# First feed-forward up projection as Strassen block products, 15 of 16 pairs of output tiles

## The chip, the cores and the metric

The kernel runs on 1 core of one Trainium2 chip. The metric is the device time of one execution, in microseconds (us). Engines: PE is TensorE, DVE is VectorE, ACT is ScalarE, POOL is GpSimd, SP is SyncE, which issues the weight loads.

## The reference

Two transformer-like layers over 512 tokens of width 1024. Only the first layer's feed-forward part is touched:

```python
h2 = rms_norm(x, norm2_w)
x = x + jnp.square(jax.nn.relu(h2 @ w_ff_in)) @ w_ff_out      # D_FF = 4096
```

All is fp32. The kernel holds activations transposed: 128 channels on the partitions, 512 tokens along the free side, so a 1024-channel activation is 8 tiles of 128x512.

## The kernel before

Every large product is a "job": one packed 128x1024 fp32 weight block (512 KB) makes one 128x512 output tile. Precision comes from splitting every factor into a rounded high part and the rest (low): a job is 8 row tiles (kt) times three matmuls, high by high, high by low, low by high, 24 matmuls of 512 columns into one PSUM bank (`block_of`, L344 to L346, called by `job`). A weight block passes four engines: SP loads it into one of four `raw` slots (L291); ACT writes the high part (`split`, L1009, 128x1024); POOL subtracts, in four pieces of 128x256 (L312); PE uses both. All queues are in order; the program is written by hand, one instruction list per engine, tied by counting semaphores.

The part around the change, in order:

- Eight jobs of the output projection (`J_OUT`). After each, DVE adds the PSUM tile to `x` (`add_to_x`), ACT squares it and makes the high part of the next input `b_hi`, DVE adds the square to `acc` and makes `b_lo` (`prep`).
- 64 feed-forward jobs: four groups g, each 8 up jobs (inputs `b_hi`, `b_lo`) and 8 down jobs (inputs `a_hi`, `a_lo`). The norm's factor `rstd` is applied after the up product: after the first up job PE sums `acc` (`norm_sum`), ACT takes the root, DVE the reciprocal (`norm_inverse`), and in the middle of the second up job (`norm_job`) PE spreads it over the partitions and ACT copies it to `rstd` (`take_rstd`). After each up job (`ff_hidden`) DVE computes relu times rstd from PSUM, ACT squares it twice, DVE subtracts to get `a_lo`. After each down job DVE adds the PSUM tile to `x` (`ff_down`).
- Then the first jobs of the second layer.

## Time and profile before

| | us |
|---|---|
| median of 3 runs | 1589.41 (1589.36 to 1590.12) |
| the profiled execution | 1589.58 |
| its span, first to last instruction | 1587.4 |
| PE busy | 1571.9 (99%) |
| POOL busy | 799.1 (50%) |
| DVE busy | 706.8 (45%) |
| ACT busy | 684.2 (43%) |

The busy time of an engine is the union of its instructions. The span is what the trace covers; the execution's own time is 2.2 us more. Matmuls overlap in the pipeline, so the duration of one (389 ns for 512 columns) is longer than the spacing of their starts, which is what counts.

### The profile page before, as it was taken

Reading aid. Unit: us, or ns where it says so; the run is one execution under the profiler, and the core shown is the slowest. Engines: PE = TensorE matmul, PEld = TensorE weight load, DVE = VectorE, ACT = ScalarE, POOL = GpSimd, SP = SyncE. Lnnn points to the kernel's source line nnn. Section 1 sums busy time; section 2 is a strip of 40 time slices with the busy share of each in tenths; the row PEclk is TensorE's granted clock in tenths of the full one; section 3 lists DMA queues with packets and bytes.
Section 4 is the critical chain, followed back from the end, with each engine's and each line's share of the span. In section 5 each row is a group of like instructions: output and inputs, shape, how many; then the busy total and the mean of one; then the engine's idle time right before and its main releaser. Section 6 shows DMA issues by size and latency. Waiting matters only on the chain. (4 is left out here: it accounts for less than half of the span.)

```text
span 1587.4 us, 22464 instructions
## 1 busy us (share of the span) xinstructions
PE 1571.9 (99%) x7602; PEld 1267.0 (80%) x7602; DVE 706.8 (45%) x1363; ACT 684.2 (43%) x1112; POOL 799.1 (50%) x1060
## 2 busy tenths in 40 slices
PE   9999999999999999999999999999999999999998
PEld 6677777777888888888887887778988888888886
DVE  5496986664233212121132446653333651552354
ACT  6435786554334423232233434543643442342333
POOL 6344654333455454545455532256544555556553
PEclk9999999999999999999999999999999999999999
DMA  5322222113232232223232421133322233233231
GB/s 196 97 94 72 86 82 75 59 57 118 94 104 93 93 106 93 94 92 106 92 106 94 132 80 53 50 111 112 114 90 96 80 106 106 80 106 106 80 106 66
DMA packets 46133, 149.91 MB, mean 94 GB/s; under 512 B 4649, under 2 KB 9905, under 8 KB 46065
## 3 DMA queue, kind: packets, MB, share of 16 engines
q1 hardware_dynamic: 39648, 140.00, 27.2%
q10 hardware_dynamic: 6416, 8.98, 1.7%
q8 instruction: 45, 0.74, 0.2%
q14 instruction: 24, 0.19, 0.0%
HBM read 146.73 MB, written 2.11 MB: 94 GB/s over the span
## 5 line engine op out<-in xcount | busy, mean ns | idle before, releaser
L312 POOL TENSOR_TENSOR w_lo<-w_raw,w_hi 128x256 fp32r<-128x256 f32 x1056 | 798.9, 789 | 765.6 <-ACT w_hi L1009 765.0
L1009 ACT ACTIVATE w_hi<-w_raw 128x1024 fp32r<-128x1024 f32 x264 | 274.9, 1051 | 293.5 <-PE job L346 284.0
L344 PE MATMUL job<-a_hi,w_hi 128*128 128x512 f32 (+1 forms) x986 | 382.4, 388 | 0.6 <-DVE a_lo L1584 0.6
L346 PE MATMUL job<-a_hi,w_lo 128*128 128x512 f32 (+1 forms) x986 | 377.3, 383 | 0.0
L345 PE MATMUL job<-a_lo,w_hi 128*128 128x512 f32 (+1 forms) x986 | 377.1, 382 | 0.0
L344 PE MATMUL job<-b_hi,w_hi 128*128 128x512 f32 x936 | 369.0, 394 | 0.8 <-DVE sq L1587 0.5
L346 PE MATMUL job<-b_hi,w_lo 128*128 128x512 f32 x936 | 364.7, 390 | 0.0
L345 PE MATMUL job<-b_lo,w_hi 128*128 128x512 f32 x936 | 364.4, 389 | 0.0
L344 PEld LDWEIGHTS job<-a_hi,w_hi 128*128 128x128 f32 x986 | 185.3, 188 | 54.8 <-issue 13.0
L346 PEld LDWEIGHTS job<-a_hi,w_lo 128*128 128x128 f32 x986 | 185.4, 188 | 36.3
L345 PEld LDWEIGHTS job<-a_lo,w_hi 128*128 128x128 f32 x986 | 185.5, 188 | 34.7
L344 PEld LDWEIGHTS job<-b_hi,w_hi 128*128 128x128 f32 x936 | 175.8, 188 | 40.4 <-issue 4.6
L346 PEld LDWEIGHTS job<-b_hi,w_lo 128*128 128x128 f32 x936 | 175.7, 188 | 36.8
L345 PEld LDWEIGHTS job<-b_lo,w_hi 128*128 128x128 f32 x936 | 175.9, 188 | 35.4 <-issue 0.2
L1587 DVE TENSOR_TENSOR arena<-arena,job 128x512 f32<-128x512 f32 (+2 forms) x89 | 60.5, 680 | 253.4 <-PE job L346 247.4
L1584 DVE SCALAR_TENSOR_TENSOR arena<-arena,vec 128x512 f32<-128x512 f32 x112 | 100.2, 895 | 60.8 <-ACT arena L1522 53.0
L1587 DVE TENSOR_TENSOR arena<-job,rstd 128x512 f32<-128x512 f32 x100 | 68.7, 688 | 130.8 <-PE job L346 108.2
L1024 ACT ACTIVATE sq<-arena 128x512 f32<-128x512 f32 x47 | 29.6, 631 | 109.4 <-DVE arena L1587 108.4
L1522 ACT ACTIVATE arena<-arena,vec 128x512 f32<-128x512 f32 x44 | 35.6, 809 | 87.4 <-DVE arena L1587 87.4
L1587 DVE TENSOR_TENSOR a_lo<-arena,a_hi 128x512 f32 (+1 forms) x58 | 40.0, 692 | 62.9 <-ACT a_hi L1270 42.2
L1269 ACT ACTIVATE arena<-arena 128x512 f32<-128x512 f32 x32 | 20.2, 632 | 106.5 <-DVE arena L1584 106.5
L1584 DVE SCALAR_TENSOR_TENSOR arena<-job,rstd 128x512 f32<-128x512 f32 x32 | 22.1, 691 | 91.2 <-PE job L346 86.6
(340 smaller groups left out, 1482.3 us busy)
## 6 DMA issues: line engine op xcount, KB each, us to landing
w_raw<-w_all SPq DMA_DIRECT2D x264, 512.0 KB, 3.4
arena<-x_t ACTq DMA_DIRECT2D x8, 512.0 KB, 5.9
out_t<-arena SPq DMA_DIRECT2D x6, 256.0 KB, 2.1
arena<-rg_w ACTq DMA_DIRECT2D x1, 1024.0 KB, 8.0
arena<-mem_t ACTq DMA_DIRECT2D x1, 1024.0 KB, 6.6
spare<-row_table ACTq DMA_DIRECT2D x3, 256.0 KB, 4.2
...
```

The lines of the kernel that those rows point to most:

```text
L312: nc.gpsimd.tensor_tensor(w_lo[:, sl, c], raw[:, sl, c], w_hi[:, sl, c].bitcast(F32), ALU.subtract).then_inc(s("lo_ready"), 1)
L344: mm(ps[:, 0:n], w_hi[:, sl, c], hi[:, kt, 0:n], start=kt == 0, stop=False)
L345: mm(ps[:, 0:n], w_hi[:, sl, c], lo[:, kt, 0:n], start=False, stop=False)
L346: ins = mm(ps[:, 0:n], w_lo[:, sl, c], hi[:, kt, 0:n], start=False, stop=kt == last)
L1009: fn(w_hi[:, sl], raw[:, sl], ACT.Copy).then_inc(s("hi_ready"), 1)
L1024: fn(sq[:, f % 2, :], src, ACT.Square).then_inc(s("sq_ready"), 1)
L1269: fn(act_s[:, c % 2, :], act_t[:, c % 2, :], ACT.Square).then_inc(s("ff_sq"), 1)
L1522: fn(f_c[u], f_u[u][:, PAD:PAD + T], ACT.Identity, scale=vcol("conv_w2", col + 88), bias=vcol("conv_b2", col)).then_inc(s("f_head"), 1)
L1584: return v.scalar_tensor_tensor(out=out_, in0=a, scalar=sc, in1=b, op0=op0, op1=op1)
L1587: return v.tensor_tensor(out_, a, b, op)
```

## The change

The first two up jobs stay as they are. The other 30 are taken in 15 pairs n (two output tiles of 128 channels). A pair's weights are a 2x2 block matrix (output tile 1 or 2, row tiles 0 to 3 or 4 to 7; W11, W12 the two tiles' upper rows, W21, W22 their lower rows), its input is a 2x2 block matrix as well (row tiles 0 to 3 or 4 to 7, token halves of 256). Seven block products in Strassen's manner (Winograd's form) take the place of eight. One block product is 4 row tiles times three matmuls of 256 columns (`ff_product`).

- Weight sums T1 = W12 - W11, T2 = W22 - T1, T3 = W22 - W12, T4 = W21 - T2 are made by POOL (`ff_sum`), each 128x512.
- Unit of weights is now 128x512 (a half of a slot): ACT makes its high part (`ff_high`), POOL the low part of raw blocks (`ff_low`, now one instruction), DVE the low part of the sums (`sum_low`). There are eight units in `w_hi` and `w_lo`; the high part of a unit waits until PE has used the one eight before. W12 alone is never multiplied.
- Input sums are made once, in four steps `combine(q)` on DVE after the last three output jobs and after the reciprocal; ACT makes their high part (`s_high`), DVE the low part.
- Output sums: three PSUM regions of 256 columns; ACT copies intermediates out (`copy_u1`, `copy_u2`, `copy_p5`) before PE adds on, DVE adds (`c11`, `c12`, `c22`), and `activate` makes the hidden tiles.
- PE's order interleaves a pair with the next: T2, W22, T3 of pair n, W11 of the next, T4 of n, W21 and T1 of the next. Pairs form four chains (1 to 3, 4 to 7, 8 to 11, 12 to 15); 8 down jobs stand between chains, and the first two down jobs are interleaved with the chain's end, on three PSUM banks in turn.
- The 64 jobs leave the numbering (`J_IN2` is now 73) and loops are written out.

```diff
+FF_JOBS = 64
+FF_CHAINS = ((1, 2, 3), (4, 5, 6, 7), (8, 9, 10, 11), (12, 13, 14, 15))
+def ff_job(n):
+    return 16 * (n // 4) + 2 * (n % 4)
+def ff_units():
+    order = [("job", 0, 0), ("job", 0, 1), ("job", 1, 0), ("job", 1, 1), None, None, None]
+    for g, chain in enumerate(FF_CHAINS):
+        order += [(w, chain[0]) for w in ("W11", "W21", "T1")]
+        for n, nxt in zip(chain, chain[1:]):
+            order += [("T2", n), ("W22", n), ("T3", n), ("W11", nxt), ("T4", n), ("W21", nxt), ("T1", nxt)]
+        n, d = chain[-1], 16 * g + 8
+        order += [("T2", n), ("W22", n), ("T3", n), ("job", d, 0), ("T4", n), ("job", d + 1, 0)]
+        order += [("job", d, 1), ("job", d + 1, 1)]
+        order += [("job", d + e, half) for e in range(2, 8) for half in range(2)]
+    return order
...
+        f_t = tiles(20, 8).rearrange("p (a i) c -> p a i c", a=2)
+        f_mid = [tiles(28, 2), spare[:, 0:2, :]]
+        f_xw = spare[:, 2, :]
+        f_s = [flat(t).rearrange("p (c t) -> p c t", t=256) for t in (tiles(28, 2), spare[:, 0:2, :])]
...
+            def ff_raw_free(f):
+                if f % 16 >= 8 or f < 2:
+                    sp.wait_ge(s("ff_raw_low"), FF_RAW["job", f, 1])
+                elif f % 2 == 0:
+                    sp.wait_ge(s("ff_sum"), FF_SUM["T4", 4 * (f // 16) + f % 16 // 2])
+                else:
+                    sp.wait_ge(s("ff_raw_low"), FF_RAW["W22", 4 * (f // 16) + f % 16 // 2])
+            for f in range(FF_JOBS):
+                if f < SLOTS:
+                    sp.wait_ge(s("lo_ready"), (J_IN2 + f - SLOTS + 1) * PIECES)
+                else:
+                    ff_raw_free(f - SLOTS)
+                sp.dma_start(ff_raw(f), w_all[J_IN2 + f]).then_inc(raw_landed[(J_IN2 + f) % SLOTS], 16)
...
+            def ff_low(*tag):
+                pool.wait_ge(s("ff_high"), FF_HIGH[tag])
+                nc.gpsimd.tensor_tensor(ff_tile(w_lo, tag), ff_source(tag), ff_tile(w_hi, tag).bitcast(F32),
+                                        ALU.subtract).then_inc(s("ff_raw_low"), 1)
+            def ff_sum(w, n, a, b):
+                if n >= 3:
+                    pool.wait_ge(s("ff_sum_low"), FF_SUMMED[w, n - 2])
+                if w in ("T2", "T4"):
+                    pool.wait_ge(s("ff_sum"), FF_SUM[w, n] - 1 if w == "T2" else FF_SUM["T2", n])
+                nc.gpsimd.tensor_tensor(ff_source((w, n)), a, b, ALU.subtract).then_inc(s("ff_sum"), 1)
...
+                for n in chain:
+                    for f in (ff_job(n), ff_job(n) + 1):
+                        pool.wait_ge(raw_landed[(J_IN2 + f) % SLOTS], 16 * ((J_IN2 + f) // SLOTS + 1))
+                    ff_sum("T1", n, ff_block("W12", n), ff_block("W11", n))
+                    ff_low("W11", n)
+                    ff_sum("T2", n, ff_block("W22", n), ff_source(("T1", n)))
+                    ff_low("W21", n)
+                    ff_sum("T3", n, ff_block("W22", n), ff_block("W12", n))
+                    ff_sum("T4", n, ff_block("W21", n), ff_source(("T2", n)))
+                    ff_low("W22", n)
...
+            def ff_product(w, n, ps, xs, first):
+                ff_wait(w, n)
+                wh, wl = ff_tile(w_hi, (w, n)), ff_tile(w_lo, (w, n))
+                for kt in range(4):
+                    c, (xh, xl) = slice(kt * P, kt * P + P), xs(kt)
+                    mm(ps, wh[:, c], xh, start=first and kt == 0, stop=False, skip_group_check=True)
+                    mm(ps, wh[:, c], xl, start=False, stop=False, skip_group_check=True)
+                    ins = mm(ps, wl[:, c], xh, start=False, stop=kt == 3, skip_group_check=True)
+                ins.then_inc(s("ff_used"), 1)
...
+            def ff_p3(n):
+                pe.wait_ge(s("ff_copied"), FF_COPY["P5", n])
+                ff_product("W22", n, ff_regions(n)[2], s_part(3), False)
+            def ff_p4(n):
+                pe.wait_ge(s("ff_part"), FF_PART["C22", n])
+                ff_product("T4", n, ff_regions(n)[0], x_part(4, 256), False)
+            def ff_p5(n):
+                if n == 1:
+                    pe.wait_ge(s("ff_part"), FF_PART["rests", 3])
+                ff_product("T1", n, ff_regions(n)[2], s_part(0), True)
+            def ff_p6(n):
+                pe.wait_ge(s("ff_copied"), FF_COPY["U1", n])
+                ff_product("T2", n, ff_regions(n)[0], s_part(1), False)
+            def ff_p7(n):
+                pe.wait_ge(s("ff_copied"), FF_COPY["U2", n])
+                ff_product("T3", n, ff_regions(n)[0], s_part(2), False)
...
+            for g, chain in enumerate(FF_CHAINS):
+                ff_p1(chain[0])
+                ff_p2(chain[0])
+                ff_p5(chain[0])
+                for n, nxt in zip(chain, chain[1:]):
+                    ff_p6(n)
+                    ff_p3(n)
+                    ff_p7(n)
+                    ff_p1(nxt)
+                    ff_p4(n)
+                    ff_p2(nxt)
+                    ff_p5(nxt)
+                ff_p6(chain[-1])
+                ff_p3(chain[-1])
+                ff_p7(chain[-1])
+                down(g, 0, 0).then_inc(s("ff_used"), 1)
+                ff_p4(chain[-1])
+                down(g, 1, 0).then_inc(s("ff_used"), 1)
+                down(g, 0, 1, (4, 5))
+                down(g, 1, 1, (4, 5))
+                down(g, 0, 1, (7, 6)).then_inc(s("ff_used"), 1)
+                down(g, 1, 1, (7, 6)).then_inc(s("ff_used"), 1)
+                for d in range(2, 8):
+                    for half in range(2):
+                        down(g, d, half).then_inc(s("ff_used"), 1)
...
+            def ff_high(*tag):
+                u = FF_UNIT[tag]
+                if tag[0][0] == "T":
+                    act.wait_ge(s("ff_sum"), FF_SUM[tag])
+                else:
+                    f = tag[1] if tag[0] == "job" else ff_job(tag[1]) + int(tag[0][2]) - 1
+                    act.wait_ge(raw_landed[(J_IN2 + f) % SLOTS], 16 * ((J_IN2 + f) // SLOTS + 1))
+                if u >= 8 and FF_ORDER[u - 8]:
+                    act.wait_ge(s("ff_used"), FF_USED[FF_ORDER[u - 8]])
+                else:
+                    act.wait_ge(s("job_done"), J_IN2 - SLOTS + u % 8 // 2 + 1)
+                fn(ff_tile(w_hi, tag), ff_source(tag), ACT.Copy).then_inc(s("ff_high"), 1)
...
+            def s_high(q):
+                act.wait_ge(s("ff_part"), FF_PART["sums", q])
+                fn(s_hi[:, :, q * 256:q * 256 + 256], f_s[q % 2], ACT.Copy).then_inc(s("ff_high"), 1)
+            def square(n, c):
+                act.wait_ge(s("ff_part"), FF_PART["act", n, c])
+                fn(act_s[:, c, :], act_t[:, c, :], ACT.Square)
+                fn(a_hi[:, 2 * (n % 4) + c, :], act_t[:, c, :], ACT.Square).then_inc(s("fhi_ready"), 1)
...
+            ff_high("W21", 1)
             norm_root(2)
-            split(J_FF + 4)
+            ff_high("T1", 1)
             take_rstd(2)
-            for c in range(8):
-                if c >= 2:
-                    split(J_FF + 3 + c)
-                ff_hidden(c % 4, 0, c // 4)
-            with act.Fori(0, 2) as i:
-                for c in range(4):
-                    split(J_FF + 11 + c, i)
-            with act.Fori(1, 3) as g:
-                with act.Fori(0, 2) as i:
-                    for c in range(4):
-                        split(J_FF + 3 + c, g * 4 + i)
-                        ff_hidden(c, g, i)
-                with act.Fori(0, 2) as i:
-                    for c in range(4):
-                        split(J_FF + 11 + c, g * 4 + i)
-            with act.Fori(0, 2) as i:
-                for c in range(4):
-                    split(J_FF + 3 + c, i + 12)
-                    ff_hidden(c, 3, i)
-
+            s_high(3)
+            ff_high("T2", 1)
+            square(0, 0)
+            square(0, 1)
...
+                ff_high("W22", a)
+                ff_high("T3", a)
+                ff_high("W11", b)
+                ff_high("T4", a)
+                copy_u1(a)
+                ff_high("W21", b)
+                ff_high("T1", b)
+                copy_p5(a)
+                for i, n in enumerate(chain[:-1]):
+                    nxt, after = chain[i + 1], chain[i + 2] if i + 2 < len(chain) else None
+                    ff_high("T2", nxt)
+                    copy_u2(n)
+                    ff_high("W22", nxt)
+                    ff_high("T3", nxt)
+                    ff_high("W11", after) if after else ff_high("job", d, 0)
+                    copy_u1(nxt)
+                    square(n, 1)
+                    ff_high("T4", nxt)
+                    ff_high("W21", after) if after else ff_high("job", d + 1, 0)
+                    square(n, 0)
+                    copy_p5(nxt)
+                    ff_high("T1", after) if after else ff_high("job", d, 1)
...
+            def combine(q):
+                part, xw = f_s[q % 2], f_xw
+                lower, upper = slice(0, 256), slice(256, T)
+                did(ts(xw, x[:, q, :], vcol("norm2", q)))
+                settle()
+                did(stt(part[:, 0], x[:, q + 4, upper], vcol("norm2", q + 4), xw[:, upper], ALU.mult, ALU.add))
+                did(tt(part[:, 2], xw[:, lower], xw[:, upper], ALU.subtract))
+                settle()
+                did(tt(part[:, 1], part[:, 0], xw[:, lower], ALU.subtract))
+                settle()
+                stt(part[:, 3], x[:, q + 4, lower], vcol("norm2", q + 4), part[:, 1], ALU.mult,
+                    ALU.subtract).then_inc(s("ff_part"), 1)
+                dve.wait_ge(s("ff_part"), FF_PART["sums", q])
+                dve.wait_ge(s("ff_high"), FF_HIGH["S", q])
+                c = slice(q * 256, q * 256 + 256)
+                tt(s_lo[:, :, c], part, s_hi[:, :, c].bitcast(F32), ALU.subtract).then_inc(s("ff_part"), 1)
...
+                if f >= 5:
+                    combine(f - 5)
...
+            def sum_low(*tag):
+                dve.wait_ge(s("ff_high"), FF_HIGH[tag])
+                tt(ff_tile(w_lo, tag), ff_source(tag), ff_tile(w_hi, tag).bitcast(F32), ALU.subtract).then_inc(
+                    s("ff_sum_low"), 1)
...
+            def c22(n):
+                part = f_mid[n % 2][:, 1, 256:T]
+                dve.wait_ge(s("ff_copied"), FF_COPY["P5", n])
+                dve.wait_ge(s("ff_used"), FF_USED["T3", n])
+                tt(part, part, ff_regions(n)[0], ALU.add).then_inc(s("ff_part"), 1)
...
+            def activate(n):
+                dve.wait_ge(s("ff_part"), FF_PART["C22", n])
+                dve.wait_ge(s("fhi_ready"), 2 * n)
+                stt(act_t[:, 1, :], f_mid[n % 2][:, 1, :], 0.0, rstd[:], ALU.max, ALU.mult).then_inc(s("ff_part"), 1)
+                stt(act_t[:, 0, 0:256], f_mid[n % 2][:, 0, 0:256], 0.0, rstd[:, 0:256], ALU.max, ALU.mult)
+                dve.wait_ge(s("ff_used"), FF_USED["T4", n])
+                stt(act_t[:, 0, 256:T], ff_regions(n)[0], 0.0, rstd[:, 256:T], ALU.max, ALU.mult).then_inc(
+                    s("ff_part"), 1)
...
+            dve.wait_ge(s("norm_root"), 2)
+            v.reciprocal(rcol[:, :, 0], rcol[:, :, 0]).then_inc(s("norm_inv"), 1)
+            combine(3)
+            dve.wait_ge(s("rstd_ready"), 2)
+            first_hidden(0)
+            sum_low("T1", 1)
+            first_hidden(1)
+            hidden_low(0, 0)
+            hidden_low(0, 1)
...
+                for i, n in enumerate(chain[:-1]):
+                    nxt, after = chain[i + 1], chain[i + 2] if i + 2 < len(chain) else None
+                    sum_low("T2", nxt)
+                    c12(n)
+                    sum_low("T3", nxt)
+                    c22(n)
+                    activate(n)
+                    hidden_low(n, 1)
+                    c11(nxt)
+                    sum_low("T4", nxt)
+                    hidden_low(n, 0)
+                    if after:
+                        sum_low("T1", after)
```

The names below: `w_hi`, `w_lo` are weight parts, `arena` and `spare` hold `x`, the sums and the intermediates, `s_hi`, `s_lo` the input sums' parts, `score` and `turn` are the PSUM regions.

DVE at the end of the output jobs, from the last output job's addition on. Before:

```order
L1587 TENSOR_TENSOR arena<-arena,job 128x512
L1587 TENSOR_TENSOR acc<-acc,sq 128x512
L1584 SCALAR_TENSOR_TENSOR b_lo<-arena,vec,b_hi 128x512
L1606 RECIPROCAL rcol<-rcol 128x4
L1584 SCALAR_TENSOR_TENSOR arena<-job,rstd 128x512
L1587 TENSOR_TENSOR a_lo<-arena,a_hi 128x512
```

With the change, from `combine(1)` (after the last but one addition) to the reciprocal:

```order
L1945 TENSOR_SCALAR spare<-arena,vec 128x512
L1938 SCALAR_TENSOR_TENSOR spare<-arena,vec,spare 128x256
L1941 TENSOR_TENSOR spare<-spare 128x256 x2
L1938 SCALAR_TENSOR_TENSOR spare<-arena,vec,spare 128x256
L1941 TENSOR_TENSOR s_lo<-spare,s_hi 128x4x256
L1941 TENSOR_TENSOR arena<-arena,job 128x512
L1941 TENSOR_TENSOR acc<-acc,sq 128x512
L1938 SCALAR_TENSOR_TENSOR b_lo<-arena,vec,b_hi 128x512
...
L1941 TENSOR_TENSOR s_lo<-arena,s_hi 128x4x256
L2304 RECIPROCAL rcol<-rcol 128x4
```

Each `combine` stands ahead of the next output job's addition or of the reciprocal.

ACT at the start of the first chain, from the input sums' last high part to the first copy out of PSUM (before, two pairs of squares stood right behind the `rstd` copy):

```order
L1560 ACTIVATE s_hi<-spare 128x4x256
L1555 ACTIVATE w_hi<-arena 128x512
L1565 ACTIVATE arena<-arena 128x512
L1566 ACTIVATE a_hi<-arena 128x512
L1565 ACTIVATE arena<-arena 128x512
L1566 ACTIVATE a_hi<-arena 128x512
L1555 ACTIVATE w_hi<-w_raw 128x512
L1555 ACTIVATE w_hi<-arena 128x512
L1555 ACTIVATE w_hi<-w_raw 128x512
L1555 ACTIVATE w_hi<-arena 128x512
L1570 ACTIVATE spare<-score 128x256
```

The last row is `copy_u1(1)`, for which PE's product T2 of pair 1 waits.

POOL within a chain: where there were four pieces of one split per job, one pair now has

```order
L446 TENSOR_TENSOR arena<-w_raw 128x512
L437 TENSOR_TENSOR w_lo<-w_raw,w_hi 128x512
L446 TENSOR_TENSOR arena<-w_raw,arena 128x512
L437 TENSOR_TENSOR w_lo<-w_raw,w_hi 128x512
L446 TENSOR_TENSOR arena<-w_raw 128x512
L446 TENSOR_TENSOR arena<-w_raw,arena 128x512
L437 TENSOR_TENSOR w_lo<-w_raw,w_hi 128x512
```

seven instructions of 128x512, in the order T1, W11, T2, W21, T3, T4, W22.

## Rows read from the trace of the kernel before

**Rows 1.** The page: busy time and granted clock.

```profile
PE 1571.9 (99%) x7602; PEld 1267.0 (80%) x7602; DVE 706.8 (45%) x1363; ACT 684.2 (43%) x1112; POOL 799.1 (50%) x1060
...
PEclk9999999999999999999999999999999999999999
```

**Rows 2.** Timeline of PE in an up or down job: start us, us, engine, line.

```profile
559.82 0.39 PE L344 MATMUL job<-a_hi,w_hi 128*128 128x512 f32 x1
...
566.84 0.39 PE L345 MATMUL job<-a_lo,w_hi 128*128 128x512 f32 x1
```

**Rows 3.** Timeline of PE, products of 256 columns.

```profile
1124.78 0.28 PE L346 MATMUL job<-a_hi,w_lo 128*128 128x256 f32 x1
...
1127.90 0.28 PE L875 MATMUL job<-w_hi,a_lo 128*128 128x256 f32 x1
```

**Rows 4.** Timeline of PE, first matmuls of 256 columns after others.

```profile
1098.24 0.36 PE L344 MATMUL job<-a_hi,w_hi 128*128 128x256 f32 x1
1098.44 0.28 PE L345 MATMUL job<-a_lo,w_hi 128*128 128x256 f32 x1
```

**Rows 5.** Groups of DVE by form: xcount | busy us, mean ns | idle before.

```profile
L1587 DVE TENSOR_TENSOR a_lo<-arena,a_hi 128x512 f32 x44 | 30.5, 693 | 51.7 <-ACT a_hi L1270 32.4 <-ACT a_hi L1527 19.3
L1591 DVE TENSOR_SCALAR arena<-arena,small 128x512 f32<-128x512 f32 x17 | 8.3, 487 | 0.6
L1587 DVE TENSOR_TENSOR arena<-job,arena 128x256 f32<-128x256 f32 x8 | 3.4, 424 | 21.3 <-PE job L346 19.0 <-ACT arena L1019 2.3
```

**Rows 6.** Groups of ACT by form.

```profile
L1009 ACT ACTIVATE w_hi<-w_raw 128x1024 fp32r<-128x1024 f32 x264 | 274.9, 1051 | 293.5 <-PE job L346 284.0 <-issue 7.3 <-DMA w_raw<-w_all 0.9
L1270 ACT ACTIVATE a_hi<-arena 128x512 f32 x24 | 14.8, 616 | 0.0
```

**Rows 7.** Timeline of ACT, a copy of 256 columns out of PSUM.

```profile
1100.75 0.38 ACT L1019 ACTIVATE arena<-turn 128x256 f32<-128x256 f32 x1 [1.13 <-PE turn L385]
```

**Rows 8.** Groups of POOL, feed-forward stretch 490 to 860 us.

```profile
L312 POOL TENSOR_TENSOR w_lo<-w_raw,w_hi 128x256 fp32r<-128x256 f32 x272 | 191.9, 737 | 179.8 <-ACT w_hi L1009 179.8
```

**Rows 9.** Timeline of POOL, one split while DVE reads PSUM or rests.

```profile
474.84 2.83 POOL L312 TENSOR_TENSOR w_lo<-w_raw,w_hi 128x256 fp32r<-128x256 f32 x4 [2.61 <-ACT w_hi L1009]
```

**Rows 10.** Timeline where DVE (two inputs in SBUF) and POOL overlap.

```profile
155.07 1.12 DVE L1584 SCALAR_TENSOR_TENSOR arena<-arena,vec 128x512 f32<-128x512 f32 x1
...
155.60 1.18 POOL L312 TENSOR_TENSOR w_lo<-w_raw,w_hi 128x256 fp32r<-128x256 f32 x1
```

**Rows 11.** Busy time of POOL by stretch: us, busy us (x pieces).

```profile
130.00:200.00 70.00, 43.24 (x43) 1.00 0.23 76
466.00:860.00 394.00, 204.19 (x290) 1.00 0.30 97
```

**Rows 12.** Timeline of DVE, last output jobs and the reciprocal.

```profile
493.60 0.69 DVE L1587 TENSOR_TENSOR arena<-arena,job 128x512 f32<-128x512 f32 x1 [2.64 <-PE job L346]
...
499.05 0.69 DVE L1587 TENSOR_TENSOR arena<-arena,job 128x512 f32<-128x512 f32 x1 [2.64 <-PE job L346]
...
504.48 0.69 DVE L1587 TENSOR_TENSOR arena<-arena,job 128x512 f32<-128x512 f32 x1 [2.64 <-PE job L346]
...
506.54 0.74 DVE L1584 SCALAR_TENSOR_TENSOR b_lo<-arena,vec,b_hi 128x512 fp32r<-128x512 f32 x1
510.94 0.18 DVE L1606 RECIPROCAL rcol<-rcol 128x4 f32<-128x4 f32 x1 [3.66 <-ACT rcol L1014]
```

**Rows 13.** Timeline of ACT, root of the norm.

```profile
507.42 1.28 ACT L1014 ACT_TABLE_LOAD   x1
510.64 0.27 ACT L1014 ACTIVATE rcol<-o,cst 128x4 f32<-128x4 f32 x1 [1.94 <-PE o L374]
```

**Rows 14.** Timeline of PE, first up job, norm sum, spread.

```profile
504.21 0.39 PE L344 MATMUL job<-b_hi,w_hi 128*128 128x512 f32 x1
...
509.66 0.95 PE L374 MATMUL o<-cst,acc 128*128 128x2 f32 x8
...
514.01 1.05 PE L385 MATMUL turn<-cst,rcol 128*128 128x128 f32 x8
```

358 lines of the change are left out of this document (266 added, 92 removed).

## The prediction

 The duration of a matmul is no price, since matmuls overlap; the price is the spacing of their starts. 31 spacings of 512 columns take 566.84 - 559.82 = 7.02 us, 0.2265 each [rows 2]; 26 spacings of 256 columns take 3.12 us, 0.1200 each [rows 3]. Then I read what the engines that feed PE can do in the time of a pair: DVE and ACT [rows 5 to 7], POOL alone [rows 8, 9], POOL against DVE [rows 10, 11], and the chain around the norm before the first pair [rows 12 to 14].
>
> **PE work.** A pair was 48 matmuls of 512 columns, 48 x 0.2265 = 10.87 us. It becomes 7 x 12 = 84 of 256 columns, 84 x 0.1200 = 10.08 us. An eighth fewer columns gives only 7%, since each start has some 13 ns that don't shrink (2 x 0.1200 - 0.2265). The saving is 0.79 us a pair, 15 x 0.79 = **11.9 us**. That is everything the change can win.
>
> The Trainium skill ("TensorE: Matmul & The Clock Gate", Back-to-back issue gap) gives the isolated gap as N / 2.4 + 2.5 ns. By it 48 x 215.8 - 84 x 109.2 ns would be 1.19 us a pair, an estimate of 17.8 us in all. The rows show 226.5 and 120.0 ns, so the measurement decides and the sum doesn't use it.
>
> **The input sums before the first pair.** One `combine` is a scale of 512 columns (0.49), four operations of 256 (0.42 as the row of that width shows, a little more for those with a factor), each but one waiting for the one before: 2.3 us. Then ACT's high part of 1024 columns, 1.05 [rows 6], then DVE's low part, twice 0.69 less one start, 1.25 [rows 5]. In all 4.6 us, and DVE's in-order queue stands still for ACT in it. An output job's own DVE work runs from the addition to the end of `b_lo` 2.8 us (504.48 to 507.28), the jobs come every 5.44 [rows 12], and 2.8 + 4.6 is 7.4. So the addition of 499.05 moves to 501.0, that of 504.48 to 508.4, the last `b_lo` to 511.2, and to 512.2 with what POOL takes from DVE (below). PE wants it for the last row tile of the first up job, 21 matmuls after 504.21 [rows 14], at 509.0: a wait of 3.2. Next, `combine(2)`, the high part, a weight split of 0.55, the table load and root of 1.28 + 0.27 [rows 13] bring the reciprocal from 510.94 to 517.85, against a wish of PE at 517.2: 0.65. `combine(3)` stands ahead of the first hidden tile, and that ahead of T1's low part, ready at 524.6; PE wants it at 523.3: 1.3. The last is on ACT: behind both hidden tiles' squares (done at 526.4) stand four splits of 0.55 and then `copy_u1(1)`, 0.38 [rows 6, 7], done at 529.0. PE's product T2 waits for it from 526.0: 3.0. The front costs 3.2 + 0.65 + 1.3 + 3.0 = **8.15 us**; without POOL's disturbance 6.5, with more of it 9.
>
> **POOL's pace.** Per pair of jobs POOL had 8 pieces of 256 columns, 8 x 0.71 = 5.7 us [rows 9]. Now it has 7 instructions of 512: three low parts and four sums. None of this width is in the trace. Bounds: two whole pieces, 2 x 0.737 = 1.47; and two spacings of 2.83 / 4 = 0.71 less one start of 0.15, as DVE saves it between 256 and 512 columns (0.424 and 0.693) [rows 5], 1.26. I take 1.30, nearer to the low end, as there is one start where there were two. Then DVE. POOL's piece takes 0.737 in the whole feed-forward stretch [rows 8], where DVE's operations read PSUM or fall into POOL's pauses. Where DVE reads two operands from SBUF, a piece takes 1.18 and the DVE operation 1.12 [rows 10], so each is held up by about 0.45; in the stretch 130 to 200 us a piece takes 43.24 / 43 = 1.0 [rows 11]. A pair has six low parts of this kind (four of sums, two of hidden tiles) and one and a half relu operations, 7.5 of 512 columns: at most 7.5 x 0.45 = 3.4 us. POOL is never idle there, so I count 0.8 of it, 2.7. A pair then costs POOL 7 x 1.30 + 2.7 = 11.8 us, 1.69 an instruction, against PE's 10.08. POOL falls behind inside a chain and catches up in the down jobs (there 2.8 of each 5.44 us).
>
> How far ahead it starts is limited by the eight unit buffers: PE at t = 0 ends the down jobs; W21 of the second pair may be split only when PE has used W11 of the first (1.44), at 2.6. From there it is the 16th POOL instruction that makes T3 of the fourth pair. Behind it come ACT's split, DVE's low part, and, in the same DVE queue, `c22` of the third pair, for which PE's T4 waits: 2.5 us. PE wants it after 21 products of 1.44 us, at 30.2. 2.6 + 16 x 1.69 + 2.5 = 32.1: **1.9 us** per chain, three chains 5.7. In the first chain there is no lead: POOL starts W22 of the first pair at 527.0, T3 of the third is its 13th, 527.0 + 22.0 + 2.5 = 551.5, and PE, from 529.0, wants it 11 products later at 544.8: **6.6 us**, in several waits (`copy_u2` behind T2's split, `c22` behind T3's low part).
>
> **What is hidden.** ACT: seven splits of 0.55, three copies of 0.38 and four squares of 0.6 are 7.4 us of 10.08. The SP queue loads the same blocks, two per pair, into four slots that come free a pair earlier than needed. The down jobs' interleaving gives `activate` of the last pair 5 us of PE work as cover; without it some 3 us per chain would be bare. That DVE's low parts are no longer hidden for POOL is counted above.
>
> **The sum.** -11.9 + 8.15 + 6.6 + 5.7 = +8.5. On the profiled execution's 1589.58 (0.2 above the median) this is **1598 us**. Low end: front 6.5, POOL at 1.26 without collisions (first chain 1, others 0): -4.4, 1585. High end: POOL at 1.47 + 0.48 = 1.95, first chain 11, others 6.6 each, front 9: +28, 1617. What a measurement of this kernel can tell from no change is 0.2%, 3.2 us.
>
> **Rivals.**
>
> 1. *POOL keeps up, faster.* If collisions are rare because DVE's operations fall between POOL's, the other chains have no wait (this decides at 1.57 us an instruction) and the first little: 1585. For it: 0.737 in rows 8. Against: POOL had pauses then and has none now.
> 2. *DVE becomes the bound.* What holds DVE in rows 10 is one piece of 256; for 512 it would be 0.45 + 0.55 = 1.0, and eight such operations a pair, 8 x 1.65 + 1.7 = 15 us, exceed even POOL. Twenty of them lie before the decisive `c22` of a chain: 37 + 1 us against 30.2, 7.5 each; the first chain 15; with the front: -11.9 + 8.2 + 15 + 22.5 = +34, 1623. Against: an operation that finds POOL between two instructions, or follows one of DVE's own, doesn't wait. The rule behind it is in the Trainium skill ("SBUF — State Buffer", Who interferes with whom): whoever issues first has the shared ports for the whole instruction, and the other fully blocks.
> 3. *The products don't do what they promise.* After other work the second matmul of 256 columns started 0.20 after the first, 0.08 late [rows 4]. If each of the 105 products began so, 8.4 us of the saving would be gone and, with the waits, the time 1606.
> 4. *No change*: front as forecast, POOL between 1.5 and 1.6 an instruction, 1588 to 1592.
>
> **How the numbers follow.** Forecast (POOL behind, 1593 to 1615) 0.56; rival 1 0.18; rival 2 0.10; rival 3 0.05; rival 4 0.11. Range 1585 to 1616: it leaves out rival 2 and half of rival 1. Slower 0.71, same 0.11, faster 0.18. The slower cases' own range is 1593 to 1618.
>
> **What would show it.** Right: matmuls of 256 columns with 0.12 between starts; before the first pair PE idle some 8 us, by `b_lo`, the spread, T1's low part and the copy out of PSUM; POOL 90% busy or more within chains at 1.6 to 1.8 an instruction; PE waiting late in each chain for DVE's addition, and early not at all. Wrong: POOL's mean under 1.5, or PE idle in the first chain under 5 us (rival 1); DVE low parts of 1.5 us and more (rival 2); starts 0.2 apart at each product's head (rival 3).

## The result, and the profile after

The change is slower: 1610.45 us, median of 4 (1610.06 to 1612.12), against 1589.47 (1589.36 to 1590.12) for the kernel before beside it. The ratio is 1.0134 [1.0121, 1.0147]: +21 us where the prediction had +8.5.

The page of the kernel after, busy time and three of its rows of tenths (a slice is 40 us):

```profile
span 1608.3 us, 23172 instructions
PE 1570.0 (98%) x8142; PEld 1290.3 (80%) x8142; DVE 844.5 (53%) x1507; ACT 739.8 (46%) x1270; POOL 872.8 (54%) x977
PE   9999999999998799999999999999999999999998
DVE  5496986654336837455473435744233651452354
PEclk9999999999999999999999999999999999999999
```

PE lost only 2 us of busy time where [rows 1] and the predicted saving ask for 12, and two slices are no longer full. The row of the clock shows nothing at this width: 9 is "90% or more". The same stretch in pieces, as start:end, length, then busy us (xcount) of PE, PEld, DVE, ACT, POOL, then the granted clock, shows it:

```profile
490.00:504.00 14.00, 14.00 (x63) 11.61 (x62) 8.54 (x13) 6.03 (x10) 6.04 (x5) 1.00 0.21 72
504.00:514.00 10.00, 5.39 (x24) 4.13 (x22) 7.95 (x11) 2.82 (x4) 4.50 (x3) 1.00 0.18 52
514.00:520.00 6.00, 5.75 (x18) 4.89 (x19) 3.90 (x9) 3.51 (x5) 1.89 (x2) 0.54 0.01 1
520.00:525.00 5.00, 5.00 (x25) 4.19 (x24) 3.98 (x5) 1.46 (x3) 2.83 (x2) 0.87 0.20 57
...
620.00:630.00 10.00, 10.00 (x87) 10.00 (x86) 10.00 (x9) 7.21 (x14) 10.00 (x7) 1.00 0.26 81
630.00:640.00 10.00, 7.32 (x49) 7.12 (x48) 8.88 (x11) 4.22 (x9) 8.84 (x7) 0.83 0.32 103
```

Two things are there: PE idle (4.6 us in 504 to 514, 2.7 in 630 to 640), and right behind each idle time a clock of 0.54, 0.87, 0.83. In the trace the granted clock goes to its lower level (1.2 instead of 2.4 GHz) from 514.46 to 521.28 and, for 3.41 us each, at 555.42, 633.92, 722.67 and 811.41. Each time PE had just waited 2.7 to 4.9 us and had taken up work again. What PE waits for between 490 and 900 us, by releaser (total, times, longest):

```profile
PE score L792 <- DVE spare L1941: 9.5, 4, 2.7
PE job L781 <- DVE b_lo L1938: 4.9, 1, 4.9
PE score L792 <- DVE arena L1941: 3.8, 4, 3.0
PE score L792 <- DVE w_lo L1941: 2.1, 1, 2.1
PE score L792 <- ACT spare L1574: 1.7, 1, 1.7
PE turn L792 <- ACT spare L1578: 0.3, 1, 0.3
```

The waits sum to 22.2 us. All but 2.0 us end with DVE. The account of PE's time closes: -11.9 saved + 22.2 waits + half of 20.5 us at half clock (6.83 + 4 x 3.41), 10.2, is **+20.5**; the spans differ by 1608.3 - 1587.4 = 20.9. Two of its terms are rough and nearly cancel. At the lower clock the spacing is 0.213 instead of 0.120 (512 columns: 0.427 instead of 0.2265), so a fall of 3.41 us costs 1.5 to 1.6 and not 1.7. And an idle time is 0.16 short, since the matmul before it counts as busy for 0.28 where its spacing is 0.12. With both, the account gives +21.4. It says where PE's time went, not what would be won if one term were gone; that is left to the experiments.

One wait and what follows it on PE, the timeline (start, us; the bracket is the idle time before and its releaser):

```profile
630.23 0.28 PE L793 MATMUL score<-b_lo,w_hi 128*128 128x256 f32 x1
630.35 0.28 PE L794 MATMUL score<-b_hi,w_lo 128*128 128x256 f32 x1
633.31 0.39 PE L792 MATMUL score<-b_hi,w_hi 128*128 128x256 f32 x1 [2.68 <-DVE spare L1941]
633.53 0.28 PE L793 MATMUL score<-b_lo,w_hi 128*128 128x256 f32 x1
...
634.27 0.42 PE L792 MATMUL score<-b_hi,w_hi 128*128 128x256 f32 x1
634.49 0.41 PE L793 MATMUL score<-b_lo,w_hi 128*128 128x256 f32 x1
```

The spacing is 0.12, as [rows 3] had it; from 634.06 on, after the wait, it is 0.21 to 0.22. The releaser is `c22(5)`, DVE's addition for the second pair of the chain of pairs 4 to 7. DVE and POOL before it:

```profile
624.38 0.41 DVE L1941 TENSOR_TENSOR spare<-spare,score 128x256 f32<-128x256 f32 x1
624.71 1.44 DVE L1941 TENSOR_TENSOR w_lo<-arena,w_hi 128x512 fp32r<-128x512 f32 x1
626.07 1.78 DVE L1941 TENSOR_TENSOR a_lo<-arena,a_hi 128x512 fp32r<-128x512 f32 x1
627.77 3.48 DVE L1941 TENSOR_TENSOR w_lo<-arena,w_hi 128x512 fp32r<-128x512 f32 x2
631.17 0.41 DVE L1941 TENSOR_TENSOR spare<-spare,turn 128x256 f32<-128x256 f32 x1
631.51 1.42 DVE L1941 TENSOR_TENSOR w_lo<-arena,w_hi 128x512 fp32r<-128x512 f32 x1
632.85 0.41 DVE L1941 TENSOR_TENSOR spare<-spare,score 128x256 f32<-128x256 f32 x1
```

```profile
613.07 1.29 POOL L437 TENSOR_TENSOR w_lo<-w_raw,w_hi 128x512 fp32r<-128x512 f32 x1 [1.81 <-ACT w_hi L1555]
614.31 1.79 POOL L446 TENSOR_TENSOR arena<-w_raw 128x512 f32<-128x512 f32 x1
...
625.56 1.74 POOL L446 TENSOR_TENSOR arena<-w_raw 128x512 f32<-128x512 f32 x1
627.25 1.75 POOL L446 TENSOR_TENSOR arena<-w_raw,arena 128x512 f32<-128x512 f32 x1
```

DVE has no gap there (10.00 of 10.00 us busy in 620 to 630). A low part that takes 0.69 alone takes 1.42 to 1.78 while POOL runs, and POOL's instruction 1.74 to 1.79 instead of 1.29. Reads out of PSUM (`score`, `turn`) keep their 0.41. T3 of pair 6 was made by POOL at 627.3 and split by ACT at 628.5 (row below); its low part starts 3.0 us later, in DVE's queue. DVE is the engine that is late.

```profile
627.87 0.63 ACT L1555 ACTIVATE w_hi<-arena 128x512 fp32r<-128x512 f32 x1 [0.57 <-PE turn L794]
```

### The profile page after: what moved, and what is told of

Its sections match the earlier page's. It is cut to its first block and busy times, and to the rows that moved or that the text cites. A ratio compares the mean times of both kernels' runs of the same rounds, so it can differ in the third digit from the quotient of the medians.

```text
span 1608.3 us, 23172 instructions
## 1 busy us (share of the span) xinstructions
PE 1570.0 (98%) x8142; PEld 1290.3 (80%) x8142; DVE 844.5 (53%) x1507; ACT 739.8 (46%) x1270; POOL 872.8 (54%) x977
## 5 line engine op out<-in xcount | busy, mean ns | idle before, releaser
L431 POOL TENSOR_TENSOR w_lo<-w_raw,w_hi 128x256 fp32r<-128x256 f32 x800 | 619.5, 808 | 595.3 <-ACT w_hi L1292 595.1
L513 PE MATMUL job<-a_hi,w_hi 128*128 128x512 f32 (+1 forms) x730 | 282.6, 387 | 1.5 <-POOL w_lo L431 1.0
L515 PE MATMUL job<-a_hi,w_lo 128*128 128x512 f32 (+1 forms) x730 | 277.6, 380 | 0.0
L514 PE MATMUL job<-a_lo,w_hi 128*128 128x512 f32 (+1 forms) x730 | 277.4, 380 | 0.0
L513 PE MATMUL job<-b_hi,w_hi 128*128 128x512 f32 x680 | 269.1, 396 | 0.9 <-DVE sq L1941 0.5
L515 PE MATMUL job<-b_hi,w_lo 128*128 128x512 f32 x680 | 265.0, 390 | 0.0
L514 PE MATMUL job<-b_lo,w_hi 128*128 128x512 f32 x680 | 264.7, 389 | 0.0
L437 POOL TENSOR_TENSOR w_lo<-w_raw,w_hi 128x512 fp32r<-128x512 f32 x113 | 163.6, 1459 | 117.6 <-ACT w_hi L1555 117.5
L1938 DVE SCALAR_TENSOR_TENSOR arena<-arena,vec 128x512 f32<-128x512 f32 (+1 forms) x114 | 101.3, 889 | 60.9 <-ACT arena L1876 53.0
L781 PE MATMUL job<-a_hi,w_hi 128*128 128x512 f32 x192 | 74.7, 389 | 0.0
```

What stands on the lines that cost most here:

```text
L431: nc.gpsimd.tensor_tensor(w_lo[:, sl, c], raw[:, sl, c], w_hi[:, sl, c].bitcast(F32), ALU.subtract).then_inc(s("lo_ready"), 1)
L437: nc.gpsimd.tensor_tensor(ff_tile(w_lo, tag), ff_source(tag), ff_tile(w_hi, tag).bitcast(F32), ALU.subtract).then_inc(s("ff_raw_low"), 1)
L513: mm(ps[:, 0:n], w_hi[:, sl, c], hi[:, kt, 0:n], start=kt == 0, stop=False)
L514: mm(ps[:, 0:n], w_hi[:, sl, c], lo[:, kt, 0:n], start=False, stop=False)
L515: ins = mm(ps[:, 0:n], w_lo[:, sl, c], hi[:, kt, 0:n], start=False, stop=kt == last)
L781: mm(ps[:], wh[:, w], hi[:, kt, :], start=kt == 0, stop=False)
```

## The experiments

The theory after the result: (A) DVE and POOL hold each other up when DVE reads two operands from SBUF, which makes DVE's queue late; PE waits; a wait of some us also drops PE's clock. Rivals to parts of it: (B) the order of DVE's queue is at fault, (C) DVE has too many instructions, whatever they read, (D) the saving of 11.9 isn't there, (E) the low clock follows from the products of 256 columns and not from the waits. "Account" below is always -11.9 + waits + half of the time at the lower clock in which PE works, against the difference of the spans; a fall that overlaps a wait counts only behind it. A chain's stretch is the time from its first product to product T4 of its last pair.

### Keeping PE busy ahead of the chain's waits

```diff
             def ff_p4(n):
+                if n in (2, 5, 9, 13):
+                    for _ in range(8):
+                        mm(t_ps[0][:], b_hi[:, 0, 0:P], b_hi[:, 0, :], start=True, stop=True)
```

> Four times (at product T4 of pairs 2, 5, 9 and 13, where PE waits 2.7 to 3.0 us for DVE) PE first does 8 matmuls of 512 columns whose result nobody reads, 1.8 us in all, so that it is idle for only about 1 us. The waits end when they did. Theory 'the idle time drops the clock': the granted clock no longer falls to half behind these four waits, which cost 3.41 us at half speed each, 1.7 us of work; the time falls by 6.8 us to about 1604 although PE does more. Rival 'only the waits cost, the clock's fall is covered by later waits': the time stays at 1610. Rival 'the clock falls for another reason (kind of product)': the falls stay and the time stays or rises.

Measured: 1614.13 us (1612.09 to 1615.53), 1.0150 [1.0133, 1.0167]. A miss: 1604 was expected. The four waits shrank to 1.21, 0.83, 0.85 and 0.86 with no fall behind them, but the next waits for DVE, 0.25 before in the last three chains, became 2.35 each (at 645.10, 735.71, 826.40), and the clock fell at those. The eight matmuls (1.81 us) ran in time that had been idle anyway: 0.83 + 1.81 is the old wait. But the fall that was gone gave nothing back. It had stood between two waits for DVE, and PE, faster now, only came to the second one earlier. The end of the chain is set by DVE's queue. The clock follows the wait to where it goes, which speaks against E. Account, with 7.2 for the 32 added matmuls: +25.2, measured 26.3.

A fall does cost where no wait for DVE stands behind it. From the first chain's last wait to the next chain's first, PE takes 78.01 us in the change (555.30 to 633.31, with a fall) and 76.51 here (555.97 to 632.48, without): 1.5 us.

### `c22` ahead of T3's low part

```diff
-                    sum_low("T3", nxt)
                     c22(n)
+                    sum_low("T3", nxt)
                     activate(n)
```

> In each pair DVE adds c22 ahead of the low part of the next pair's T3, not behind it; nothing else moves. Theory 'DVE's queue order': PE's T4 waits (1.44, 3.03, 2.68, 2.69, 2.67 us, 12.5 in all) shrink to a few tenths, and with them four clock falls of 1.7 us go: 1610.5 - 12.5 - 6.8 = 1591, up to 1596 where new waits come behind. Rival 'POOL's pace is the bound': POOL needs some 11.8 us a pair against PE's 10.1 whatever DVE's order is, the waits come back at T3 or W22 of the later pairs, and the time stays above 1600.

Measured: 1609.24 (1607.43 to 1609.99), 1.0120 [1.0103, 1.0137]. The 2.68 became 1.82, and a second 1.82 appeared at `c22` of the next pair where 0.26 had been. The waits sum to 23.8. A miss: 1591 to 1596 was expected. What DVE does later it does at PE's expense all the same. B falls as a cause of the chains' waits. The account, +18.4, is 2.4 short of the measured 20.8; that is the largest gap of all runs here, in the one with the most waits, and it stays unexplained.

The run shows once more what a fall in a chain costs. The stretch of a chain in the change (a fall between two waits), then here without a fall and with one behind the last wait:

```profile
698.97:745.23 46.26, 43.32 (x338) 42.44 (x337) 37.27 (x43) 28.02 (x54) 38.61 (x26) 0.96 0.28 87
```

```profile
697.71:743.77 46.06, 42.15 (x337) 41.07 (x336) 37.44 (x43) 27.26 (x54) 38.36 (x25) 1.00 0.27 86
786.03:833.59 47.56, 43.70 (x337) 42.60 (x336) 36.89 (x43) 26.66 (x53) 38.10 (x26) 0.96 0.27 89
```

Between two waits for DVE the fall is covered (46.26 against 46.06). The one with no wait behind it costs 1.5 us.

### DVE's low parts of the sums, 8 columns wide

```diff
-                tt(ff_tile(w_lo, tag), ff_source(tag), ff_tile(w_hi, tag).bitcast(F32), ALU.subtract).then_inc(
+                tt(ff_tile(w_lo, tag)[:, 0:8], ff_source(tag)[:, 0:8], ff_tile(w_hi, tag)[:, 0:8].bitcast(F32),
+                   ALU.subtract).then_inc(
```

> Leaves out most of the low parts of the weight sums on DVE: 8 of 512 columns are made, so the products of the sums are computed with wrong low parts. DVE then has four operations a pair less, and POOL is held up less. Theory 'DVE and POOL hold each other up': POOL's mean for 512 columns falls from 1.5 towards 1.35 us, DVE is idle again in the chains, the waits at T4 go, and the time is about 1610 - 12.5 - 6.8 = 1591. Rival 'POOL alone is too slow': POOL's own 7 x 1.27 = 8.9 us a pair plus the rest keeps it behind, waits of 2 us stay, 1600 or more.

Measured: 1588.35 (one run; 1591 was expected), span 1586.6. No wait is left in the last three chains, only

```profile
PE job L781 <- DVE b_lo L1938: 4.9, 1, 4.9
PE score L792 <- ACT spare L1570: 1.9, 1, 1.9
PE score L792 <- ACT spare L1574: 0.8, 1, 0.8
```

and one fall (514.21 to 521.04). Account: -11.9 + 7.6 + 3.2 = -1.1, measured 1586.6 - 1587.4 = -0.8. This frees DVE of work and POOL of collisions at once, so it doesn't tell A from C.

### The same low parts at full width, first operand from PSUM

```diff
-                tt(ff_tile(w_lo, tag), ff_source(tag), ff_tile(w_hi, tag).bitcast(F32), ALU.subtract).then_inc(
+                tt(ff_tile(w_lo, tag), t_ps[0][:], ff_tile(w_hi, tag).bitcast(F32), ALU.subtract).then_inc(
```

The low parts subtract from what lies in that PSUM bank instead of from the sums; count, width and waits are those of the change.

> DVE's low parts of the weight sums are of the same number and width, but their first input is read from a PSUM tile (t_ps[0]) and not from SBUF, so the sums' products are computed with wrong low parts. Theory 'two inputs in SBUF against POOL': DVE's operation takes 0.69 us whatever POOL does, POOL's mean for 512 columns falls to about 1.4, the chain waits go as with the narrow low parts, and the time is near that kernel's 1588. Rival 'DVE simply has too many operations': the waits at T4 stay above 1 us and the time above 1600.

Measured: 1588.97 (1588.49 to 1589.37), 0.9996 [0.9987, 1.0006]. Groups between 490 and 860 us (xcount | busy us, mean ns | idle before), of the change and then of this kernel:

```profile
L437 POOL TENSOR_TENSOR w_lo<-w_raw,w_hi 128x512 fp32r<-128x512 f32 x113 | 163.6, 1459 | 117.6 <-ACT w_hi L1555 117.5
L446 POOL TENSOR_TENSOR arena<-w_raw 128x512 f32<-128x512 f32 x30 | 46.6, 1555 | 0.0
L446 POOL TENSOR_TENSOR arena<-w_raw,arena 128x512 f32<-128x512 f32 x30 | 46.2, 1542 | 0.0
L1941 DVE TENSOR_TENSOR w_lo<-arena,w_hi 128x512 fp32r<-128x512 f32 x60 | 67.5, 1140 | 6.1 <-ACT w_hi L1555 5.7
```

```profile
L446 POOL TENSOR_TENSOR arena<-w_raw 128x512 f32<-128x512 f32 x30 | 42.6, 1419 | 0.0
L446 POOL TENSOR_TENSOR arena<-w_raw,arena 128x512 f32<-128x512 f32 x30 | 40.6, 1353 | 0.0
L1941 DVE TENSOR_TENSOR w_lo<-turn,w_hi 128x512 fp32r<-128x512 f32 x60 | 40.3, 686 | 14.0 <-ACT w_hi L1555 13.8
```

As many DVE instructions of the same width, 0.69 instead of 1.14 us each, and the last three chains have no wait of 0.1 us or more. The stretch of a chain is 41.3 us, against 46.3 in the change: DVE's lateness costs 4.9 a chain. So C falls: it is not the number of DVE's instructions but where their operands lie. The Trainium skill ("SBUF — State Buffer", Who interferes with whom) says that a DVE instruction with at most one SBUF input, outside the 2-port modes, doesn't contend with GpSimd, and that one with two contends with a GpSimd instruction that reads SBUF. The trace agrees, with 686 against 1140 ns.

### The saving by itself

The sums on POOL and the low parts on DVE 8 columns wide; `combine` in two halves, so that DVE doesn't stand still for ACT; root and `copy_u1(1)` earlier:

```diff
-                nc.gpsimd.tensor_tensor(ff_source((w, n)), a, b, ALU.subtract).then_inc(s("ff_sum"), 1)
+                nc.gpsimd.tensor_tensor(ff_source((w, n))[:, 0:8], a[:, 0:8], b[:, 0:8], ALU.subtract).then_inc(
+                    s("ff_sum"), 1)
...
+                if f >= 6:
+                    rests_of(f - 6)
...
-                    combine(f - 5)
+                    sums_of(f - 5)
```

> Leaves out most of the weight sums on POOL and of their low parts on DVE (8 of 512 columns each; the sums' products then use wrong weights), and takes the input sums apart so that DVE's queue no longer stands still for ACT's high part, the norm's root ahead of the third high part, the first copy out of PSUM ahead of four splits. PE's products are all there. Theory 'the saving is 0.79 us a pair, the rest is waits and clock': 1589.5 - 11.9 + 1 or 2 for what is left of the front = 1579. Rival 'the products themselves cost more than their spacing (restarts at each of 105 products, 0.08 each)': 1587 or more without any long wait.

Measured: 1583.79 (1582.91 to 1584.24), 0.9963 [0.9949, 0.9978]. Two waits remain (2.32 for `b_lo`, 2.41 for T2's low part) and one fall of 3.41: -11.9 + 4.7 + 1.7 = -5.5, measured 1581.1 - 1587.4 = -6.3. The time is 4.8 above the 1579 expected, by what is left of the front. D falls: the products save what [rows 2, 3] say, within 0.8 us. E falls too: the same products of 256 columns run at the full clock everywhere but behind the front's wait.

### The hidden tiles' operands in PSUM

The two relu operations read `rstd` from the PSUM bank in which PE spread it, and ACT writes the squares for `a_lo` to a PSUM bank:

```diff
-                fn(act_s[:, c, :], act_t[:, c, :], ACT.Square)
+                if n > 0:
+                    act.wait_ge(s("flo_ready"), 2 * n + 1 - c)
+                elif c > 0:
+                    act.wait_ge(s("flo_ready"), 1)
+                fn(o_ps[:], act_t[:, c, :], ACT.Square)
...
-                stt(act_t[:, 1, :], f_mid[n % 2][:, 1, :], 0.0, rstd[:], ALU.max, ALU.mult).then_inc(s("ff_part"), 1)
-                stt(act_t[:, 0, 0:256], f_mid[n % 2][:, 0, 0:256], 0.0, rstd[:, 0:256], ALU.max, ALU.mult)
+                stt(act_t[:, 1, :], f_mid[n % 2][:, 1, :], 0.0, t_ps[0][:], ALU.max, ALU.mult).then_inc(
+                    s("ff_part"), 1)
+                stt(act_t[:, 0, 0:256], f_mid[n % 2][:, 0, 0:256], 0.0, t_ps[0][:, 0:256], ALU.max, ALU.mult)
...
-                tt(a_lo[:, h, :], act_s[:, c, :], a_hi[:, h, :].bitcast(F32), ALU.subtract).then_inc(
+                tt(a_lo[:, h, :], o_ps[:], a_hi[:, h, :].bitcast(F32), ALU.subtract).then_inc(
```

> Nothing is left out. The relu reads rstd from the PSUM tile where PE had spread it, and ACT writes the squares that DVE only subtracts from into the PSUM bank o_ps; so 3.5 of 7.5 DVE operations of 512 columns a pair no longer read two inputs in SBUF. Theory as above: POOL per pair falls from 12 to 10.5 us and DVE's held operations from 8 to 4; the waits of 2.7 to 3.0 us at T4 and the clock falls behind them go, 1595 to 1600 is left (the front before the first chain is unchanged). Rival 'the four weight low parts alone keep DVE behind': 1605 or more.

Measured: 1594.87 (1594.33 to 1595.58), 1.0034 [1.0022, 1.0047]. The low end of what was expected (1595 to 1600). Nothing is left out of the computation here, and 15.6 us of the change's 21 are gone. The waits of the last three chains are 0.3 us each, with no fall; `a_lo` takes 681 ns on average where it took 1258. The low parts of the sums still read SBUF twice (1164 ns). So not every collision has to go, only enough of them for DVE to keep up.

### The front, and the parts put together

A first order of the front stood in the run of "The saving by itself". A second one: the input sums an output job earlier, so that on ACT their high part (`s_high`) stands ahead of the next job's square, and `rests_of` and `sums_of` behind `b_lo`; root, T1's low part and `copy_u1(1)` earlier as well:

```diff
-                if f >= 5:
-                    s_high(f - 5)
+                if f == 7:
+                    norm_root(2)
+                if f >= 4:
+                    s_high(f - 4)
```

> Nothing is left out. The input sums are made one output job earlier, their low parts one job later than the sums, so that DVE doesn't stand still for ACT; the norm's root and reciprocal come ahead of the last ones; the first copy out of PSUM ahead of four splits. The chains are as they were. Theory 'the front costs its waits and a double clock fall': 4.85 + 3.4 us at the last row tile of the first up job and some 2 us at T1 go, about 1600. Rival 'the first chain is bound by POOL from a fixed start, so a faster front only waits later': 1606 to 1610.

Measured: 1612.45 (1611.70 to 1613.42), 1.0145 [1.0128, 1.0162]. A miss (about 1600 expected): the wait for `b_lo` grew from 4.9 to 7.6, since the high part and a split on ACT (511.95 to 513.5) stood ahead of the square that DVE's `acc` waits for. The waits behind it shrank (2.08 to 1.17), the chains stayed at 2.64. In the last chain no fall followed the 2.64, and its next wait is 2.33 instead of 0.19 to 0.24: its stretch is 46.81 without a fall, 46.22 in the chain before with one.

A third one: an input sum in every second output job only, its sums in one step and its low part in the next, the other two behind the last job; on ACT the splits of W22 and T3 of pair 1 ahead of the squares:

```diff
-                if f >= 5:
-                    combine(f - 5)
+                if f in (4, 6):
+                    sums_of(f // 2 - 2)
+                if f in (5, 7):
+                    rests_of(f // 2 - 2)
+            sums_of(2)
```

> Nothing is left out. Only as much of the input sums stands between the output jobs as DVE has time for: sums 0, low part 0, sums 1, low part 1, one after each of the last four; the others behind the last b_lo, with the norm's root and reciprocal between; on ACT the splits of W22 and T3 and the first copy come ahead of squares. The chains' own order is unchanged. If the front is a cost by itself: the wait of 4.85 us with its double clock fall (3.4) and most of the first chain's early waits go, 1600. If the chains' T4 waits are bound by POOL and DVE from their own starts they stay (2.7 each).

Measured: 1606.83 (1604.94 to 1607.83), 1.0104 [1.0088, 1.0119]. The wait for `b_lo` is 2.64, and the fall behind it 3.41 instead of 6.83 us. The expected 1600 was missed: the chains kept their waits, 2.6 to 2.7 and in one a second of 2.35.

The second front, the hidden tiles in PSUM, `c22` first and, on ACT, `copy_u2` ahead of T2's split, together; the last of these edits is

```diff
-                    ff_high("T2", nxt)
                     copy_u2(n)
+                    ff_high("T2", nxt)
```

> Nothing is left out. front2 and psum_hidden together, c22 ahead of T3's low part, and the copy of the second intermediate ahead of the split of T2. If waits and clock falls are all that stood against the saving of 11.9 us: 1589.5 - 11.9 + 2 to 4 for what is left in the first chain, 1580 to 1582, faster than before and after. If POOL's pace still binds inside chains: 1585 to 1592.

Measured: 1591.63 (1591.09 to 1592.46), 1.0013 [1.0004, 1.0023]. Not the 1580 to 1582 of the theory but the rival's 1585 to 1592. One wait of 7.58 is most of the 10.6 that are left, and the clock was low for 13.65 us around it.

The same with the third front, which leaves nothing out of the computation; on ACT that is

```diff
-                if f >= 5:
-                    s_high(f - 5)
+                if f in (4, 6):
+                    s_high(f // 2 - 2)
...
-            ff_high("W21", 1)
             norm_root(2)
+            s_high(2)
+            ff_high("W21", 1)
+            s_high(3)
```

> Nothing is left out. front3 with the chain changes of best (squares and rstd read from PSUM, c22 and the copy of the second intermediate ahead). The run best kept two waits in the front (7.6 and 1.2 us) and a clock fall of 13.7 us; without these 1591.6 - 8 - 6 = 1578 to 1582, faster than the kernel before by 0.5%.

Measured: **1585.61** (1585.12 to 1586.19), **0.9974 [0.9963, 0.9984]**, faster than both kernels, by 0.26% against the kernel before, though slower than the 1578 to 1582 expected. What PE still waits for, and two stretches of it:

```profile
PE job L781 <- DVE b_lo L1948: 2.6, 1, 2.6
PE turn L792 <- ACT spare L1582: 2.4, 1, 2.4
PE score L792 <- ACT spare L1574: 0.3, 1, 0.3
PE turn L792 <- DVE w_lo L1951: 0.2, 1, 0.2
```

```profile
510.00:530.00 20.00, 16.07 (x91) 13.89 (x91) 18.49 (x23) 10.47 (x18) 10.48 (x8) 0.91 0.18 53
630.00:640.00 10.00, 10.00 (x84) 9.92 (x83) 6.05 (x11) 7.02 (x15) 8.11 (x6) 1.00 0.44 136
```

Account: -11.9 + 5.5 + half of the two falls of 3.41 as far as PE works in them, 3.3, is -3.1; measured 1583.9 - 1587.4 = -3.5. Only the four waits at the front are left. The 2.4 is `copy_p5(1)`, behind four splits in ACT's queue; moving it ahead of them wasn't tried.

### The price of the clock by itself, in the kernel before

Three waits put into the kernel before (first output tile of three up jobs waits for the hidden tile just before it):

```diff
+                if c in (3, 5, 7):
+                    pe.wait_ge(s("flo_ready"), c)
```

> The kernel before, with one thing added: ahead of up jobs 3, 5 and 7 PE waits until DVE has finished the low part of the hidden tile made just before, a wait of about 2.7 us (0.17 + 0.69 + 1.2 + 0.69) that nothing else in that stretch hides or lengthens. Theory 'a wait of this length lets the clock fall to half': up to three falls of 3.4 us behind the waits, each 1.7 us more: 1589.6 + 8.1 + 5.1 = 1602.8. Rival 'only the wait costs': 1597.7.

and the same with eight matmuls into an unused bank ahead of each:

```diff
+                if c in (3, 5, 7):
+                    for _ in range(8):
+                        mm(s_ps[2][:], b_hi[:, 0, 0:P], b_hi[:, 0, :], start=True, stop=True)
+                    pe.wait_ge(s("flo_ready"), c)
```

> As idle_waits, but PE does 8 matmuls of 512 columns ahead of each of the three waits, 1.8 us whose result nobody reads, so the wait ends when it did but PE is idle for only 0.9 us. Theory 'the idle time drops the clock': no falls, 1597.7. Rival 'the falls have another cause, or come with any wait': as idle_waits.

Measured: 1600.78 (1599.18 to 1600.90) and 1598.58 (1598.28 to 1599.16), 1.0067 [1.0051, 1.0082] and 1.0055 [1.0040, 1.0070]. The first two waits of each:

```profile
524.00:530.00 6.00, 4.44 (x12) 3.53 (x13) 0.69 (x1) 1.73 (x3) 3.04 (x5) 0.72 0.29 97
539.00:545.00 6.00, 3.92 (x17) 3.24 (x18) 0.81 (x2) 2.10 (x3) 2.82 (x4) 1.00 0.27 87
```

```profile
524.00:530.00 6.00, 5.12 (x23) 3.90 (x22) 0.78 (x2) 2.10 (x3) 3.60 (x6) 1.00 0.29 90
539.00:545.00 6.00, 5.12 (x23) 4.17 (x23) 0.69 (x1) 1.12 (x2) 2.83 (x4) 1.00 0.33 97
```

With the same data to wait for, but PE idle 0.88 instead of 2.69 us, the kernel is 2.2 us faster and the clock doesn't fall at all. In the profiled execution of the kernel with idle waits it fell once, behind the first (526.52 to 529.93), and not behind the other two, as long. So idle time lowers the clock also without any product of 256 columns, and E is gone; how often a wait of this length does is not settled. The spans, 1598.5 and 1597.0, differ by 1.5 us; the spacing in the fall, 0.427 instead of 0.2265 us, makes 1.6. The Trainium skill ("TensorE: Matmul & The Clock Gate", HAM oscillation) describes a kernel in which every wait between short stretches of matmuls is followed by work at the lower clock. The trace agrees that waits lower the clock, but here, with 11 to 13 us of work between waits of 2.69, only one in three did.

## Why the prediction was wrong in size

The direction and the engines were right, the size was not: +8.5 against +21. By its own steps:

- **PE work, -11.9: right.** Spacings of 0.12; the accounts of the runs with few waits come within 0.8 us of it.
- **Front, 8.15: 7.3, but otherwise made up, so the match is luck.** The wait for `b_lo` was 4.85, not 3.2: "with what POOL takes from DVE" counted 1.0 us, and `acc` and `b_lo` alone came out at 1.61, 1.77 and 1.55 where [rows 12] have about 0.7. The reciprocal's 0.65 and the 1.3 for T1's low part never came, since PE itself was late by then. The wait for `copy_u1(1)`, forecast as 3.0, was 2.08: the copy ended at 531.87 and T2's low part, which the trace names as the releaser, at 531.94. A further copy cost 0.3.
- **First chain, 6.6: 6.15** (1.68 + 1.44 + 3.03), with the names given (`copy_u2`, `c22`). Part of this is luck too: POOL started at 530.1, not 527.0, its T3 of pair 3 was ready at 551.0 instead of 549.0, and from there to `c22` it took 4.3 instead of 2.5; but PE was later as well.
- **The step that failed: three further chains at 1.9 each, of which the 2.5 us from POOL's T3 to `c22`.** A chain lost 4.9 (a stretch of 46.3 against 41.3 without waits). POOL's pace was right: 12 starts from 614.31 to 632.34 are 1.64 an instruction, forecast 1.69. The path behind it was not. I followed POOL, ACT and then DVE as if DVE were free, and charged the collisions in the chains to POOL alone. By the same working T3 of the third pair is the 9th instruction, and `c22` of the second pair would be done at 2.6 + 9 x 1.69 + 2.5 = 20.3, just when PE wants it (14 x 1.44 = 20.2). POOL was even a little early, at 16.9 (627.30 - 610.45), but `c22` took 6.0 us from there: the split T3 lay ready 3.0 us while DVE worked off its queue. So the larger wait came a pair earlier than forecast, and `c22` of the third pair at 34.9 instead of 32.1. Of the 4.9, 2.9 are idle (2.68 + 0.25) and most of the rest is work at the lower clock, which DVE's lateness would have turned into waiting otherwise.
- **A term put at nothing: TensorE's clock.** I read 0.998 for the kernel before, in which PE never waits in this stretch, and took it over to a kernel with a forecast of 20 us of waits. Where no wait for DVE covers a fall it cost 1.5 behind the first chain and, by the spacing, 3.2 behind the wait for `b_lo`: 4.7. Whether those 3.2 would all come back is not shown.

Together 8.5 + 9.1 (three chains, 14.8 instead of 5.7) + 4.7 (clock) - 1.3 (waits of front and first chain, 13.4 instead of 14.75) = +21.0, measured 20.9. That the waits sum to 22.2 where 20.45 was forecast says little, since DVE's lateness shows as idle time in one place and as low clock in another.

The range's high end was also added up wrong: with 1.95 an instruction the same working gives 10.0 for the first chain and 6.1 for each other one, not 11 and 6.6, so 1615 instead of 1617.

Rivals: 1 fell, although its sign came true (POOL's mean is 1.48 us an instruction over the feed-forward part, but 1.64 where it matters, and PE lost 6.15 in the first chain); 3 fell, by the run with the sums narrow and by the accounts; 4 fell with the time. 2 had the right engine and about two thirds of its 7.5 us a chain; its sign, low parts of 1.5 us and more, held for 18 of the 60, while 26 took 0.68 to 0.69. What decides in the chains is that DVE and POOL block each other: with the same number of instructions and one operand in PSUM, their loss is gone.
